# GpSimd's arithmetic moves to VectorE, and eight small loads to GpSimd's queue, in a fused two-block transformer kernel

## What is computed

```python
def hybrid_mixer(h, w_in, conv_w, conv_b, conv_ln_g, conv_ln_b, w_out):
    proj = h @ w_in
    q, k, v, a, g = jnp.split(proj, [...], axis=-1)
    attn = moba_attention(heads(q), heads(k), heads(v))
    u = a * jax.nn.sigmoid(g)
    u = causal_depthwise_conv(u, conv_w, conv_b)     # 31 taps, 1024 channels
    u = jax.nn.silu(layer_norm(u, conv_ln_g, conv_ln_b))
    mix = jnp.concatenate([attn, u], axis=-1)
    return mix @ w_out
```

## Time and profile before

| | |
|---|---|
| median of three runs | 2973.56 us |
| profiled execution, its span | 2976.3 us |
| TensorE busy (matmul) | 2643.6 us, 89% |
| VectorE busy | 1989.9 us, 67% |
| ScalarE busy | 1245.7 us, 42% |
| GpSimd busy | 297.9 us, 10% |
| DMA, mean over the span | 209 GB/s |
| chain that ended last | PE 70%, DVE 13%, DMA 8%, issue 5%, ACT 2% |

### The profile page before, as it was taken

The page is one execution under the profiler, slowest core; times in us unless marked ns, Lnnn a source line. Parts: engine busy times, 40 slices in busy tenths (PEclk is TensorE's granted clock), DMA queues, the critical chain, the costliest instruction groups (busy, mean ns, idle before and its releaser), DMA issues.

```text
span 2976.3 us, 45692 instructions
## 1 busy us (share of the span) xinstructions
PE 2643.6 (89%) x16246; PEld 2368.8 (80%) x16246; DVE 1989.9 (67%) x2197; ACT 1245.7 (42%) x1733; POOL 297.9 (10%) x227
## 2 busy tenths in 40 slices
PE   0768667889999999999899999998889999999998
PEld 0668566669999999888787877776679999998886
DVE  5758989675768874698465555554777776656554
ACT  1225554444333333344452433333345555554443
POOL 0445744001200000000000000000000000000000
PEclk9978888889999999999899999999989999999999
DMA  7757645578987866787434545442858876655654
GB/s 265 265 204 256 203 156 191 207 273 243 282 294 249 273 206 183 261 285 265 141 128 161 161 154 169 144 157 84 296 198 270 275 224 184 183 174 172 191 193 144
DMA packets 239299, 622.70 MB, mean 209 GB/s; under 512 B 20123, under 2 KB 24955, under 8 KB 238106
## 3 DMA queue, kind: packets, MB, share of 16 engines
q1 hardware_dynamic: 232988, 603.12, 61.2%
q0 software_dynamic: 4432, 11.56, 1.9%
q10 hardware_dynamic: 1788, 6.80, 0.7%
HBM read 613.79 MB, written 7.60 MB: 209 GB/s over the span
## 4 chain that ended last, share of the span: by engine, by line
PE 70%; DVE 13%; DMA 8%; issue 5%; ACT 2%; ACTq 1%; SPq 0%; DVEq 0%; POOL 0%; POOLq 0%
PE ps L1601 11%; PE ps L1602 11%; PE ps L1603 11%; PE ps L1789 5%; PE ps L1790 5%; PE ps L1791 5%; PE ps L1577 5%; PE ps L1579 5%; PE ps L1578 5%; DVE w_lo L1019 3%; DVE acc L1026 3%; DVE ff L1203 2%; DMA ada<-in_ada_w 2%; DVE acc L1112 2%; DMA start<-in_ada_w 2%
## 5 line engine op out<-in xcount | busy, mean ns | idle before, releaser
L1019 DVE TENSOR_TENSOR w_lo<-raw,w_hi 128x1024 fp32r<-128x1024 f32 x742 | 935.9, 1264 | 707.2 <-ACT w_hi L625 701.3
L625 ACT ACTIVATE w_hi<-raw 128x1024 fp32r<-128x1024 f32 x766 | 811.1, 1060 | 1329.2 <-PE ps L1603 467.6
L1601 PE MATMUL ps<-h_hi,w_hi 128*128 128x256 f32 x3296 | 953.7, 289 | 57.5 <-DVE w_lo L1019 32.8
L1602 PE MATMUL ps<-h_lo,w_hi 128*128 128x256 f32 x3296 | 946.4, 287 | 0.0
L1603 PE MATMUL ps<-h_hi,w_lo 128*128 128x256 f32 x3296 | 945.9, 287 | 0.0
L1601 PEld LDWEIGHTS ps<-h_hi,w_hi 128*128 128x128 f32 x3296 | 647.4, 196 | 63.8 <-DVE w_lo L1019 35.9
L1602 PEld LDWEIGHTS ps<-h_lo,w_hi 128*128 128x128 f32 x3296 | 647.2, 196 | 1.1 <-issue 0.7
L1603 PEld LDWEIGHTS ps<-h_hi,w_lo 128*128 128x128 f32 x3296 | 646.6, 196 | 0.0
L1026 DVE SCALAR_TENSOR_TENSOR acc<-ada,cact,acc 128x1024 f32<-128x1024 f32 x320 | 448.1, 1401 | 18.6 <-DMA ada<-in_ada_w 16.3
L1789 PE MATMUL ps<-w_hi,f_hi 128*128 128x512 f32 x952 | 379.6, 399 | 34.5 <-DVE f_lo L1244 33.7
L1790 PE MATMUL ps<-w_lo,f_hi 128*128 128x512 f32 x952 | 375.7, 395 | 0.0
(11 more groups left out here) (157 smaller groups left out, 2275.2 us busy)
## 6 DMA issues: line engine op xcount, KB each, us to landing
ada<-in_w_ada SPq DMA_DIRECT2D x192, 512.0 KB, 4.2
raw<-in_ffn_w_up SPq DMA_DIRECT2D x160, 512.0 KB, 4.0
ada<-in_ada_w SPq DMA_DIRECT2D x128, 512.0 KB, 4.0
raw<-in_na_w_qkv SPq DMA_DIRECT2D x96, 512.0 KB, 4.6
raw<-in_w_gate SPq DMA_DIRECT2D x88, 512.0 KB, 4.9
raw<-in_w_up SPq DMA_DIRECT2D x88, 512.0 KB, 4.7
raw<-in_w_down SPq DMA_DIRECT2D x88, 512.0 KB, 5.0
raw<-in_ffn_w_down SPq DMA_DIRECT2D x86, 512.0 KB, 3.7
```

Source lines behind the costliest of these rows:

```text
L625: act.activation(w_hi[:, s, :], raw[:, s, :], ACT.Copy).then_inc(hi_ready, 1)
L1019: dve.tensor_tensor(w_lo[:, s, :], raw[:, s, :], w_hi[:, s, :].bitcast(F32), ALU.subtract).then_inc(lo_ready, 1)
L1601: pe.matmul(o, w_hi[:, s, a], h_hi[:, k, :], start=(k == 0 and g % 2 == 0), stop=False)
L1602: pe.matmul(o, w_hi[:, s, a], h_lo[:, k, :], start=False, stop=False)
```

## The change

GpSimd does no tensor-tensor arithmetic any more.

- The 24 low parts of START are VectorE's: 0 to 3 of each half behind its 32 steps, tiles 4 to 11 between steps 5 to 19 of half 1 (behind every odd one), the rest one ahead of each of the eight early units.
- ScalarE's products come in rounds: 31 rounds of four groups (0 to 3), then 31 of two (4 and 5), in two slots of `taps` of four groups each. VectorE adds each round in one instruction, 30 of 128x1024 and 30 of 128x512 (`conv_sums`). Both sides take 3 rounds ahead of the q chunk, then one and two rounds in turn per step. VectorE's own taps begin earlier, in the q chunk.
- The eight small loads move from ScalarE's queue to GpSimd's, behind its memsets.
- `taps` and `post1` move in SBUF; `conv_pool` becomes `conv_add`.

```diff
         st_fc = at("st_fc", [86, 4, P], 133 * KB)
-        taps = at("taps", [P, 6, SEQ], 170 * KB)
+        taps = at("taps", [P, 2, 4, SEQ], 168 * KB)
...
         scr = [at("scr0", [P, TILE], E + 4 * KB), at("scr1", [P, TILE], E + 20 * KB)]
-        post1 = at("post1", [P, D], 162 * KB)
+        post1 = at("post1", [P, D], 160 * KB)
         post2 = at("post2", [P, D], E + 8 * KB)
...
         conv_prod = sem("conv_prod")
-        conv_pool = sem("conv_pool")
+        conv_add = sem("conv_add")
         std_ready = sem("std_ready")
...
-        CONV_PRODUCTS = [(tap, pair) for tap in range(TAPS) for pair in range(2)] + [(tap, 2) for tap in range(TAPS)]
-        CONV_SUMS = 3 * (TAPS - 1)
+        CONV_ROUNDS = [(tap, 0, 4) for tap in range(TAPS)] + [(tap, 4, 6) for tap in range(TAPS)]
+        CONV_ADDS = 2 * (TAPS - 1)
+
+        def conv_rounds(step):
+
+            return 1 + step % 2
+
         DVE_CONV = (6, 7)
...
-            for j in range(START_TILES):
-
-                pool.wait_ge(hi_ready, T_AG + j + 1)
-                pool.tensor_tensor(w_lo[:, j % RING, :], raw[:, j % RING, :], w_hi[:, j % RING, :].bitcast(F32),
-                                   ALU.subtract).then_inc(lo_ready, 1)
-
+            for n, name in enumerate(("conv_b", "conv_ln_g", "conv_ln_b")):
+                pool.dma_start(st_c24[H1 * n:H1 * (n + 1), :], ins[name].rearrange("a (r n) -> (a r) n", n=P))\
+                    .then_inc(small_landed, 16)
+            pool.dma_start(st_cw[:, :], ins["conv_w"][0]).then_inc(small_landed, 16)
+            pool.dma_start(st_fc[:, 0:3, :], ins["ffn_conv_w_2"][0].rearrange("t (r n) -> r t n", n=P)).then_inc(small_landed, 16)
+            pool.dma_start(st_fc[:, 3, :], ins["ffn_conv_b_2"][0].rearrange("(r n) -> r n", n=P)).then_inc(small_landed, 16)
+            pool.dma_start(qg[:, :], ins["na_q_g_2"][0:1, :].to_broadcast([P, HD])).then_inc(small_landed, 16)
+            pool.dma_start(kg[:, :], ins["na_k_g_2"][0:1, :].to_broadcast([P, HD])).then_inc(small_landed, 16)
...
             pool.memset(u_pad[:, :, 0:TAPS - 1], 0.0).then_inc(const_ready, 1)
-
-
-            def add_product(a, r, pair, ahead, behind):
-
-                dst = ff[:, H1 + 2 * pair:H1 + 2 * pair + 2, :]
-                pool.wait_ge(conv_prod, a + (ahead + 1))
-                pool.wait_ge(conv_pool, a + (3 - behind))
-                pool.tensor_tensor(dst, dst, taps[:, 2 * (r % 3):2 * (r % 3) + 2, :], ALU.add).then_inc(conv_pool, 1)
-
-            with pool.Fori(0, 2 * (TAPS - 1) // 6) as i:
-                for r in range(6):
-                    add_product(i * 6 + r, r, r % 2, 2, 2)
-            with pool.Fori(2 * (TAPS - 1) // 3, CONV_SUMS // 3) as i:
-                for r in range(3):
-                    add_product(i * 3 + r, r, 2, 3, 1)
-
...
             act.dma_start(x[:, :, :], ins["x"][0].rearrange("(t p) d -> p t d", p=P)).then_inc(x_landed, 16)
-            for n, name in enumerate(("conv_b", "conv_ln_g", "conv_ln_b")):
-                act.dma_start(st_c24[H1 * n:H1 * (n + 1), :], ins[name].rearrange("a (r n) -> (a r) n", n=P))\
-                    .then_inc(small_landed, 16)
-            act.dma_start(st_cw[:, :], ins["conv_w"][0]).then_inc(small_landed, 16)
-            act.dma_start(st_fc[:, 0:3, :], ins["ffn_conv_w_2"][0].rearrange("t (r n) -> r t n", n=P)).then_inc(small_landed, 16)
-            act.dma_start(st_fc[:, 3, :], ins["ffn_conv_b_2"][0].rearrange("(r n) -> r n", n=P)).then_inc(small_landed, 16)
-            act.dma_start(qg[:, :], ins["na_q_g_2"][0:1, :].to_broadcast([P, HD])).then_inc(small_landed, 16)
-            act.dma_start(kg[:, :], ins["na_k_g_2"][0:1, :].to_broadcast([P, HD])).then_inc(small_landed, 16)
-
-
             act.wait_ge(tr_done[0], 1)
...
-            products = [0, 0]
+            rounds = [0, 0]
...
-
                 for _ in range(times):
-                    if products[0] == len(CONV_PRODUCTS):
+                    if rounds[0] == len(CONV_ROUNDS):
                         return
-                    tap, pair = CONV_PRODUCTS[products[0]]
-                    a = products[1]
-                    products[0] += 1
-                    products[1] += tap > 0
-                    if tap and a >= 3:
-                        act.wait_ge(conv_pool, a)
-                    for c in (2 * pair, 2 * pair + 1):
+                    tap, c0, c1 = CONV_ROUNDS[rounds[0]]
+                    a = rounds[1]
+                    rounds[0] += 1
+                    rounds[1] += tap > 0
+                    if tap and a >= 2:
+                        act.wait_ge(conv_add, a - 1)
+                    for c in range(c0, c1):
                         dst, src, wv = conv_operands(c, tap)
...
                         else:
-                            s = act.activation(taps[:, a % 3 * 2 + c % 2, :], src, ACT.Copy, scale=wv)
+                            s = act.activation(taps[:, a % 2, c - c0, :], src, ACT.Copy, scale=wv)
                     s.then_inc(conv_prod, 1)
...
                 if n > 4:
-                    conv_products(2)
+                    conv_products(1)
             sigmoid_of_g(START_TILES + CT)
...
             for n in range(CT):
-                conv_products(1)
                 hi(T_QKV1, n + 3)
-                conv_products(1)
+                conv_products(conv_rounds(n))
             act.wait_ge(pair_free[2], 2)
...
                 for n in range(CT, 2 * CT):
-                    conv_products(1)
                     hi(T, n + 3)
-                    conv_products(1)
+                    conv_products(conv_rounds(n))
                 chunk_wait(T, 2 * CT)
...
                         act.activation(tmp[:, :], ff[:, 8:16, :].rearrange("p g n -> p (g n)"), ACT.Square).then_inc(sq_ready, 1)
-                    conv_products(1)
                     hi(T, n + 3)
-                    conv_products(1)
+                    conv_products(conv_rounds(n))
                 chunk_wait(T, 3 * CT)
...
                     hi(T, 3 * CT + u + 3)
-                    conv_products(2)
+                    conv_products(conv_rounds(u))
...
-                assert products[0] == len(CONV_PRODUCTS)
+                assert rounds[0] == len(CONV_ROUNDS)
                 attention(PER_GROUP, M["att1"], NT, lambda h: slice(GH + h, GH + h + 1), lambda u: None)
...
                                              in1=a, op0=ALU.mult, op1=ALU.add).then_inc(start_step, 1)
+                    if s and o % 2 and 4 < o - HOPS < 5 + 2 * (HTILES - RING):
+                        lo(T_AG, RING + (o - HOPS - 5) // 2)
                 if s == 0:
...
+                for n in range(RING):
+                    lo(T_AG, HTILES * s + n)
                 m_ = M["start"] + 3 * s
...
             for n in range(EARLY_UNITS):
+                lo(T_AG, START_TILES - HTILES + RING + n)
                 mixer_unit(n)
-            dve.wait_ge(lo_ready, START_TILES + RING)
             for j in range(3):
...
             dve.wait_ge(const_ready, 5)
-            taps_done = [0]
+            taps_done = [0, 0, 0]
+
+            def conv_sums(times):
+
+                for _ in range(times):
+                    if taps_done[1] == len(CONV_ROUNDS):
+                        return
+                    tap, c0, c1 = CONV_ROUNDS[taps_done[1]]
+                    taps_done[1] += 1
+                    if tap == 0:
+                        continue
+                    a = taps_done[2]
+                    taps_done[2] += 1
+                    dve.wait_ge(conv_prod, taps_done[1])
+                    if a:
+                        dve.wait_ge(conv_add, a)
+                    dst = ff[:, H1 + c0:H1 + c1, :]
+                    dve.tensor_tensor(dst, dst, taps[:, a % 2, 0:c1 - c0, :], ALU.add).then_inc(conv_add, 1)
...
+            conv_sums(CT - 5)
             for n in range(CT):
...
                 mixer_unit(EARLY_UNITS + CT + n)
+                conv_sums(conv_rounds(n))
+                if n > 1:
+                    conv_taps()
             dve.wait_ge(pair_free[2], 2)
...
                         dve.tensor_copy(stat[:, 62:63], ps[:, 6, 0:1]).then_inc(tr_free[0], 1)
-                    conv_taps()
                     lo(T, n + 3)
...
                     mixer_unit(EARLY_UNITS + CT + 3 * CT * i + n)
+                    conv_sums(conv_rounds(n))
+                    conv_taps()
...
                     lo(T, 3 * CT + u + 3)
+                    mixer_unit(EARLY_UNITS + 4 * CT + u)
+                    conv_sums(conv_rounds(u))
                     conv_taps()
-                    mixer_unit(EARLY_UNITS + 4 * CT + u)
...
                     gate_rows(M["a_g1"], post1)
-            assert taps_done[0] == DVE_CONV_OPS
+            assert taps_done == [DVE_CONV_OPS, len(CONV_ROUNDS), CONV_ADDS]
             dve.wait_ge(tr_free[1], M["ln"] + 1)
...
             pe.sem_inc(ada_used, 2 + 2 * UNITS)
-            pe.sem_inc(conv_pool, 2)
             for s in pair_free:
...
```

(2 more changed lines are left out.)

## The result

| | kernel before | kernel after |
|---|---|---|
| median (lowest to highest) | 2971.8 us (2966.3 to 2978.3) | 2909.9 us (2908.1 to 2911.7) |
| span of the profiled execution | 2976.3 us | 2908.6 us |
| time after / before | | 0.9785, 95% interval 0.9771 to 0.9799 |

The medians are of four runs each. The change gives 62 us by the medians, 67.7 by the spans of the two profiled executions; the profiled execution of before, 2978.3 us, was the longest of its four and lay 6.5 us above their median. The forecast was 2913 us.

What follows compares the result with a forecast made beforehand. VectorE was taken to set the pace during the convolution, its instructions stretched by GpSimd's. The terms sum to 60.2 us off 2976.3, giving 2916.1; less 2.7 for the profiled execution, 2913 us. Range 2892 to 2943.

Steps and rivals of the forecast that it cites:

- Steps 1 and 2: Start: small loads on GpSimd's queue end idle DMA time, 13.6 us; then half 0's last three units run unstretched, 2.8 us.
- Step 3: Half 1 of START: VectorE takes eight low parts between its units, which lose their stretched form; gain 8 us.
- Step 4: Last 12 tiles of START: VectorE's faster low parts and short units let SyncE issue tiles earlier; gain 6.5 us.
- Step 5: Second chunk (a1): VectorE would be free in time for its multiply after the sigmoid; gain 2.7 us.
- Steps 6 and 7: Convolution: the q chunk loses 0.9 us to the new sums; the next 16 steps gain 4.8 us.
- Step 8: First attention, 8 units: short instructions plus narrow sums make a unit 6.3 us; gain 6.7 us.
- Step 9: Second QKV group up to the mean: gain 16 us, where VectorE alone would save 19.
- The start gives back: Rival, 0.20: SyncE's queue order eats gains in START's half 1 and last 12 tiles, sums wait for products; 2937 us.
- More comes back: Rival, 0.08: upper bounds reached in the start and, at 19 us, the second QKV group; 16 us more, 2897 us.
- Late small loads: Rival, 0.06: small loads on GpSimd's queue come too late for ScalarE's first rounding; 7 to 10 us lost, 2922 us.
- `cact` not earlier: Rival, 0.04: in the start, the 2 MB load of x alone blocks ScalarE's queue, so the small-load gain goes; 2927 us.
- the stretched form does not come from GpSimd: Rival, 0.04: DMA or ScalarE traffic stretches VectorE's instructions, so they stay stretched, 54 us more between 254 and 509 us; 3011 us.

Runs made afterwards that it cites:

- The last run: Kernel after, with each START half's first four tile loads behind its last adaLN loads and low parts of tiles 4 to 11 two steps earlier: 2903.2 us.

## Why the prediction was right

The sum was 60.2 us, and at the mean, where it was to be complete, the trace shows 66.1. The steps are read from the milestones above; its reading of the page holds but for "its highest", as slice 18 has a 9 too.

- *Steps 1 and 2*: 16.4 forecast, 15.3 measured. By the two pairs that differ in the small loads alone, step 1 is 10.0 to 12.4 us, not 13.6; by the two pairs of traces that differ in the low parts alone, step 2 is 2.5 to 2.9. The price of step 1 came from idle DMA time, and that held: the window's DMA share rose from 0.32 to 0.87. A by-product of it did not. "The first adaLN step near 13 us" took for granted that the weights would be there as soon as `cact`; they landed at 19.93. The DMA engines were 0.97 busy from 5 to 20 us, with the 2 MB of x (landed 11.0 us after its issue) beside the first weights; that this sharing made them late is the likely cause, not a tested one. The gain was the same, since it was priced by transfers and not by that start.
- *Step 3*: 8 forecast, 9.0 measured (84.1 against 75.1 us). The stepping gave 76.
- *Step 4*: 6.5 and 7.2. *Step 5*: 2.7 and 1.7.
- *Steps 6 and 7*: 3.9 forecast, 7.8 measured. Here is an error of arithmetic. Step 7 priced all its 24 sums as wide, beside the 14 of step 6, 38 of the 30 there are. The trace has 16 wide and 7 narrow ones between 267 and 340.8 us: 16 x 1.14 + 7 x 0.60 = 22.4 us instead of 27.4, so 5 us too little gain. The 16 steps take 73.7 us, not 78.3.
- *Step 8*: 6.7 and 6.2. The unit was priced at 6.3 us and takes 6.4.
- *Step 9*: 16 forecast, 18.9 measured. The prediction had 19 for VectorE alone and cut it, because TensorE's own work was read as 40.1 of 58 us. That reading was of a window with a granted clock of 0.91. In the kernel after the same stretch is granted 1.00, and TensorE was no bound:

```profile
394.10:430.50 36.40, 34.15 (x236) 31.10 (x236) 36.09 (x48) 18.71 (x31) 0.00 (x0) 1.00 0.74 234
```

  The same stretch of before, cut at its own ends (441.4 to 496.6 us), has TensorE at 37.1 us with a clock of 0.89. VectorE is still what sets the pace here, 36.09 of 36.40 us.
- *Mean and subtraction*: 12.7 forecast, 12.4 measured. The mean's matmuls run at 0.379 us where the median one took 0.634; the granted clock was 0.58 in their 6.5 us before, behind 7.82 us of idle time, and is 1.00 now, with no idle time ahead. It changes little, since VectorE has four low parts with units between the start of the mean and the subtraction now, and had three.
- *Behind it*: 66.4 us at the subtraction of the mean and 67.7 at the end. The lead lies mostly between 64 and 68 us on the way, with no place of its own.

Steps 6 and 7 were too small by 3.9 us and step 9 by 2.9; the others differ by 1.1 us or less each in these two traces. But the start of the profiled execution of before was itself late: the kernel with the sums alone runs the same program up to the first sigmoid, 4.8 us sooner. Against that trace the kernel after gains 26.8 us by the first sigmoid, where steps 1 to 4 add up to 30.9. So the forecast had the start some 4 us too high, and steps 5 to 9 (29.3 forecast, 34.6 measured) 5 us too low, and the two nearly cancel. Without those 4.8 us the 66.1 at the mean would be 61.3, in line with the 62 between the medians. The mechanism held in every step; that the time came within 3 us of 2913 is in part luck.

The rivals. *The start gives back*: the order of SyncE's queue did not eat steps 3 and 4, but its mechanism is in the trace. Tiles 4 to 7 went out at 72.61 us and the next four start loads at 76.43, behind them; these were in time, as VectorE ran its next eight steps from 87.60 us on without a wait. The pair behind them was not: it went out at 96.43, behind tile 8 (96.02), which waited for low part 4 (94.77), and VectorE waited 2.69 us at 102.21 and 1.27 at 104.77. The last run shows that some 7 to 8 us lay in that order and in the place of the low parts. VectorE did not wait for products at all: its 2.0 us of idle time ahead of the sums are 19 times 0.10 us between two sums that follow each other, which the prediction had allowed for. The 0.6 us of room was enough. ScalarE waited 30.6 us in 24 places for the sums, which cost next to nothing, since VectorE was busy 111.2 of the 112.8 us from 228 to 340.8:

```profile
L712 ACT ACTIVATE taps<-u_pad,cvec x180: 490/494/518, 222.2 to 420.0; 128x256 f32<-128x256 f32 x180
...
  DVE ff L1187: 30.6, 24
```

*More comes back* named step 9's 19 us rightly; its other terms stayed at the middle. *Late small loads* did not come: their transposes began 12.7 us after the last issue (8.84 to 21.5), with 36 us of cover. By the prediction's reading of the page of the Trainium skill that it quotes, VectorE's opening memsets could have starved them of descriptors; the passage names fast modes and doesn't say that a memset is one. The second memset runs from 3.51 to 5.27 us. The issues follow each other without a gap from 3.05 to 8.84 us, and the first three, issued up to 4.77, landed 1.8 to 2.0 us later, so no run here shows such a stall. The larger loads behind them took 5.7 to 13.2 us to land, while the DMA engines were 0.97 busy. *`cact` not earlier* is refuted by two runs, and *the stretched form does not come from GpSimd* by the run with unneeded adds.

## What to carry to other kernels

Where an engine is full, compare the durations of one and the same instruction before counting instructions. If it has two forms, find which engine is busy in one and idle in the other; here 57 us of new work on the fullest engine paid for itself, because it ended meetings that cost it 85. When a bound is read from an engine that was itself waiting, its clock in that window belongs to the reading, and when instructions are shared out among steps, add them up again at the end.

## What the hardware showed beyond the expectation

- A VectorE instruction with two operands in SBUF that meets a GpSimd instruction which reads SBUF is held up by that instruction's least recorded duration less 0.2 to 0.3 us: for a unit or a tap 2.13 us beside low parts of 2.333, 1.03 beside adds of 1.261, 0.78 beside 1.038, 0.139 beside 0.397. It doesn't depend on its own length (a tap of 0.477 us and a unit of 1.277 pay the same 0.78), and low parts and sums pay 0.04 to 0.06 us more.
- 288 memsets of 128x512 on GpSimd at 0.526 us each, beside the same VectorE work, don't lengthen the forms with two SBUF operands (1218, 1277 and 477 ns as without them), but they do lengthen those with one: a TENSOR_SCALAR of 353 ns has a mean of 489 and takes up to 787.
- A queue of ScalarE that holds x and five small loads takes its next small load 19.2 us long, in all three traced kernels that have it there (from 7.41, 7.47 and 7.36 us on), and everything ScalarE has to compute stands behind it. GpSimd's queue took eight such loads at 0.52 to 0.69 us each, the one of 258 rows at 1.89. Which limit ScalarE's queue had met was not tried.
